# The last group of down products and the final norm in column chunks of 512, 512 and 26 instead of three of 350

## The chip, the cores and the metric

The kernel runs on one core of a Trainium2 chip. The metric is the device time of one execution in microseconds, the median of several. Engines are named TensorE (PE in the profile; PEld for its weight loads), VectorE (DVE), ScalarE (ACT), GpSimd (POOL) and SyncE (SP, which only issues transfers).

## The reference

One step of a decoder layer with D = 1024 for 1,050 tokens at once: 16 meta tokens, 1,024 prompt tokens, 8 sample tokens and 2 columns of padding. After two mixing branches (RG-LRU and gated linear attention) and their output projection comes the feed-forward part, and then the final norm. The change touches only the end of this:

```python
xn2 = rmsnorm(x, norm2_g)
u = xn2 @ w_ffn_up                      # 1024 -> 6144
uc = causal depthwise conv(u)
gate, val = split(uc, 2)
x = x + (gelu(gate) * val) @ w_ffn_down # 3072 -> 1024
y = x * rsqrt(mean(x * x) + 1e-6) * final_norm_g
```

All is float32. The outputs are y and the states of the branches and convolutions.

## The kernel before, in words

Activations are kept with the model dimension on the partitions: a block is 128 dimensions x C = 1050 token columns of float32, and the model dimension makes KB = 8 blocks. Every large product is made of three float32r products (high x high, high part of the weights x low part of the data, low x high), since weights and data are split into a high and a low part. GpSimd splits the weights (L366, L368), SP loads them (512 KB units). Columns go in three chunks of NW = 350, one PSUM bank each: `acc` is two groups of three banks, and two small banks are left, `sb6` and `sb7`.

The feed-forward part goes in 8 groups of GRP = 3 blocks of d_ff. For each group `up` makes gate and value, VectorE and ScalarE form the activation, and `down` adds the group's product to the residual X2, one 1050-column block at a time (L399 by way of `tile_products`; the add is L1502). The down products of the last group are done differently, and this is the part that changes. Their weights stand in SBUF split in full (`lhi`, `llo`, 3 units), so the loops are turned: columns outside, blocks inside. Chunk n = 0, 1, 2; in it block m = 0..7; in it 3 x 3 products of 350 columns (L737), into one bank per block (`last_bank(m)`, 8 banks). What follows is pipelined behind it by semaphores:

- VectorE adds the bank to X2 (L1540), and one block later adds the square to the running sum `ysum` (L1535; a copy, L1532, for block 0). These stand in one order in VectorE's program: add of block t, then sum of block t - 1.
- ScalarE squares the new X2 into one of two halves of `ysq` (L1092) and writes X2 x final_norm_g to Y (L1093).
- TensorE sums `ysum` over the partitions with a product by a matrix of ones, in fp32 (L422, called by `final_sum`). For chunk n - 1 this stands in TensorE's program after block 2 of chunk n, for the last chunk after its end. A bank is written again in chunk n once the add of the same block of chunk n - 1 is done; block 7 also waits for the Ln of chunk n - 1, because the ones product uses its bank.
- ScalarE makes the factor `yrs` (Ln, L1081, and Exp, L1084), in its program after block 2 of the next chunk.
- The scale Y x yrs is done by GpSimd for chunks 0 and 1, 8 blocks each (L391), and by VectorE for chunk 2 (L1551), after all its sums.
- SP stores y: one transfer for all 8 blocks of chunk 0, one for chunk 1 (L351), each after GpSimd's 8 scales, then four of two blocks for chunk 2 (L354). SP's program is in this order, and each transfer is queued behind the ones before it. At the end SP waits for all stores.

A row of y in memory is 1,050 floats, so a store of a chunk is made of one piece per partition and block, as long as the chunk is wide: 1,400 bytes for 350 columns.

Of the kernel before, what the change touches and what calls it, by code (L numbers as in the profile page):

```python
# [28 lines left out]
P = 128  # L29
D = 1024  # L30
# [24 lines left out]
EPS = 1e-6  # L55
TINY = 2.0 ** -63


# [44 lines left out]
def build(nc, I, O):  # L103
    ctx = ExitStack()
    with ctx:
# [105 lines left out]
        Y = at("y", M0, KB * C)  # L211
        ysq, ysum, yrs = at("y_square", F0, 2 * NW), at("y_square_sum", F0 + TB, C), at("y_rms", F0 + 2 * TB, C)

# [100 lines left out]
        def _(sp):  # L314
# [33 lines left out]
            Y3, y_out = Y.rearrange("p (k c) -> p k c", k=KB), O["y"].rearrange("k p c -> p k c")  # L348
            for n in range(2):
                sp.wait_ge(y_pool_done, KB * (n + 1))  # L350
                sp.dma_start(y_out[:, :, n * NW:(n + 1) * NW], Y3[:, :, n * NW:(n + 1) * NW]).then_inc(y_stored, 16)  # L351
            for k in range(0, KB, 2):
                sp.wait_ge(y_done, k + 2)
                sp.dma_start(y_out[:, k:k + 2, 2 * NW:], Y3[:, k:k + 2, 2 * NW:]).then_inc(y_stored, 16)  # L354
            sp.wait_ge(y_stored, 16 * (2 + KB // 2))
            sp.wait_ge(stored, 16 * 6)
# [3 lines left out]
        def _(pool):  # L360
# [25 lines left out]
            for n in range(2):  # L386
                c = slice(n * NW, (n + 1) * NW)
                pool.wait_ge(r3_done, n + 1)
                for m in range(KB):
                    pool.wait_ge(yg_done, KB * n + m + 1)  # L390
                    nc.gpsimd.tensor_tensor(blk(Y, m)[:, c], blk(Y, m)[:, c], yrs[:, c], ALU.mult).then_inc(y_pool_done, 1)  # L391

        @block.tensor
        def _(pe):
# [326 lines left out]
            def final_sum(n):  # L721
                pe.wait_ge(sum3_done, KB * (n + 1))
                pe.wait_ge(last_added, KB * (n + 1))
                norm_sum(ysum, n, last_bank(KB - 1), sum3_mm)
            for n in range(3):
                for m in range(KB):
                    if n == 0 and m in (2, 5):
# [5 lines left out]
                    for k in range(GRP):  # L733
                        v, t = divmod(m * GRP + k, KB)
                        b = (GRP + k) * C + n * NW
                        for w, x, a, z in ((lhi, AH, k == 0, False), (lhi, AL, False, False), (llo, AH, False, k == GRP - 1)):
                            mm = nc.tensor.matmul(last_bank(m)[:, 0:NW], w[v][:, t * P:(t + 1) * P], x[:, b:b + NW],  # L737
                                                  start=a, stop=z)
# [6 lines left out]
        def _(act):  # L745
# [332 lines left out]
            def final_factor(n):  # L1078
                c = slice(n * NW, (n + 1) * NW)
                act.wait_ge(sum3_mm, n + 1)  # L1080
                nc.scalar.activation(yrs[:, c], last_bank(KB - 1)[:, 0:NW], ACT.Ln, scale=1.0 / D, bias=cst[:, 0:1])\  # L1081
                    .then_inc(lnr3_done, 1)
                act.wait_ge(lnr3_done, n + 1)
                nc.scalar.activation(yrs[:, c], yrs[:, c], ACT.Exp, scale=-0.5).then_inc(r3_done, 1)  # L1084
            for n in range(3):
                c = slice(n * NW, (n + 1) * NW)
                for m in range(KB):
                    t = KB * n + m
                    act.wait_ge(last_added, t + 1)
                    if t >= 2:  # L1090
                        act.wait_ge(sum3_done, t - 1)
                    nc.scalar.activation(ysq[:, t % 2 * NW:(t % 2 + 1) * NW], blk(X2, m)[:, c], ACT.Square).then_inc(sq3_done, 1)  # L1092
                    nc.scalar.activation(blk(Y, m)[:, c], blk(X2, m)[:, c], ACT.Identity, scale=par("gf", m)).then_inc(yg_done, 1)  # L1093
                    if n > 0 and m == 2:
                        final_factor(n - 1)
# [3 lines left out]
        def _(dve):  # L1099
# [427 lines left out]
            def square_sum(t):  # L1527
                n, m = divmod(t, KB)
                c, q = slice(n * NW, (n + 1) * NW), ysq[:, t % 2 * NW:(t % 2 + 1) * NW]
                dve.wait_ge(sq3_done, t + 1)  # L1530
                if m == 0:
                    nc.vector.tensor_copy(ysum[:, c], q).then_inc(sum3_done, 1)  # L1532
                else:
                    dve.wait_ge(sum3_done, t)
                    nc.vector.tensor_tensor(ysum[:, c], ysum[:, c], q, ALU.add).then_inc(sum3_done, 1)  # L1535
            for n in range(3):
                c = slice(n * NW, (n + 1) * NW)
                for m in range(KB):
                    dve.wait_ge(last_mm, KB * n + m + 1)
                    nc.vector.tensor_tensor(blk(X2, m)[:, c], last_bank(m)[:, 0:NW], blk(X2, m)[:, c], ALU.add)\  # L1540
                        .then_inc(last_added, 1)
                    if KB * n + m > 0:
                        square_sum(KB * n + m - 1)
                if n < 2:
                    continue
                square_sum(3 * KB - 1)

                dve.wait_ge(r3_done, 3)
                for m in range(KB):
                    dve.wait_ge(yg_done, KB * n + m + 1)  # L1550
                    nc.vector.tensor_tensor(blk(Y, m)[:, c], blk(Y, m)[:, c], yrs[:, c], ALU.mult).then_inc(y_done, 1)  # L1551

# [110 lines left out]
```

## Time and profile before

| what | value |
|---|---|
| median of 3 runs | 1990.11 us (1988.91 to 1990.44) |
| profiled execution: span | 1984.4 us |
| profiled execution: own time | not given apart from the span |
| mean granted TensorE clock | 0.989 of full |
| moved by DMA | 127.38 MB |

Times in the profile are microseconds from the span's start, on the one core. A line such as "L737 PE MATMUL acc<-act_hi,last_hi" is the line of the kernel, the engine, the operation and the names of output and inputs; "x54" is how many. A product's duration is longer than its spacing to the next, since they overlap in the array; spacings of starts tell the pace. A TensorE product in fp32 is recorded as two instructions. PEclk is the granted TensorE clock (1.00 is 2.4 GHz, 0.50 is 1.2 GHz).

### The profile page before, as it was taken

What the parts mean: (1) busy time and instruction counts of PE and PEld (TensorE: products, weight loads), DVE (VectorE), ACT (ScalarE), POOL (GpSimd) and SP (SyncE); (2) the same over time, 40 slices, a digit from 0 to 9 for tenths busy, and PEclk for the clock granted to TensorE, in tenths of its full rate; (3) what the DMA queues carried; (4) which work ended last, traced back from release to release, by engine and by line L of the source; (5) the groups of instructions that cost most, each with busy time, mean ns of one, the idle gap of its engine ahead of it and who ended that gap; (6) DMA issues with size and microseconds to landing.
All of it is one profiled execution on the core that took longest, in us unless ns stands there. A gap on an engine that the chain in (4) does not pass through costs nothing.

```text
span 1984.4 us, 29047 instructions
## 1 busy us (share of the span) xinstructions
PE 1932.3 (97%) x11890; PEld 1904.1 (96%) x11890; DVE 911.0 (46%) x918; ACT 422.9 (21%) x480; POOL 702.0 (35%) x324
## 2 busy tenths in 40 slices
PE   7999999999999999999999999999999999999997
PEld 6999888888889999999999999999999999999997
DVE  5211277877865311141234455536253535354546
ACT  4000154555532100020021221101010201010115
POOL 2333222322234333343443333334333333333353
PEclk9999999999999999999999999999999999999999
DMA  5221123222211111131122111111111111111112
GB/s 191 86 89 43 44 97 110 77 90 77 77 68 49 49 47 42 56 127 42 42 80 103 55 43 43 54 43 43 44 54 43 43 44 53 44 43 43 54 51 87
DMA packets 48167, 127.38 MB, mean 64 GB/s; under 512 B 6952, under 2 KB 19880, under 8 KB 48080
## 3 DMA queue, kind: packets, MB, share of 16 engines
q1 hardware_dynamic: 27744, 88.52, 13.5%
q10 hardware_dynamic: 20352, 37.78, 5.4%
q8 instruction: 61, 1.00, 0.2%
q14 instruction: 10, 0.08, 0.0%
HBM read 108.23 MB, written 18.31 MB: 64 GB/s over the span
## 4 chain that ended last, share of the span: by engine, by line
PE 92%; DVE 4%; issue 3%; ACT 1%; DMA 0%; DVEq 0%; SPq 0%
PE acc L399 84%; PE acc L576 1%; PE acc L737 1%; PE small L496 1%; PE small L499 1%; DVE rg_xc_h L1307 1%; PE small L508 1%; DVE rg_xc_h L1304 1%; PE small L471 0%; DVE rg_ext L1129 0%; PE small L737 0%; PE small L589 0%; DVE gla_bc_keT L1194 0%; DMA x_in<-in_x 0%; PE small L515 0%
## 5 line engine op out<-in xcount | busy, mean ns | idle before, releaser
L366 POOL TENSOR_TENSOR w_hi<-w_raw,ones 128x1024 fp32r<-128x1024 f32 x149 | 288.0, 1933 | 1232.2 <-PE acc L399 1220.5
L399 PE MATMUL acc<-xn_hi,w_hi 128*128 128x350 f32 x2520 | 558.9, 330 | 15.2 <-DVE xn_lo L1117 11.2
L399 PE MATMUL acc<-xn_lo,w_hi 128*128 128x350 f32 x2520 | 546.7, 325 | 0.0
L399 PE MATMUL acc<-xn_hi,w_lo 128*128 128x350 f32 x2520 | 544.1, 324 | 0.0
L399 PEld LDWEIGHTS acc<-xn_hi,w_hi 128*128 128x128 f32 x2520 | 430.4, 191 | 21.0 <-issue 13.1
L399 PEld LDWEIGHTS acc<-xn_lo,w_hi 128*128 128x128 f32 x2520 | 432.7, 190 | 0.0
L399 PEld LDWEIGHTS acc<-xn_hi,w_lo 128*128 128x128 f32 x2520 | 432.1, 190 | 0.0
L368 POOL TENSOR_TENSOR w_lo<-w_raw,w_hi 128x1024 fp32r<-128x1024 f32 x149 | 384.3, 2579 | 11.7
L1502 DVE TENSOR_TENSOR residual<-acc,residual 128x1050 f32<-128x1050 f32 x56 | 70.0, 1250 | 117.0 <-PE acc L399 117.0
L1473 DVE SCALAR_TENSOR_TENSOR tmp<-val_ext,ffn_params,tmp 128x1040 f32<-128x1040 f32 x48 | 98.1, 2044 | 39.8 <-ACT tmp L1049 37.0
L1473 DVE SCALAR_TENSOR_TENSOR gate_conv<-gate_ext,ffn_params,gate_conv 128x1040 f32<-128x1040 f32 x48 | 92.1, 1920 | 41.0 <-ACT gate_conv L1043 38.1
L399 PE MATMUL acc<-act_hi,w_hi 128*128 128x350 f32 x504 | 108.9, 325 | 0.0
L399 PE MATMUL acc<-act_lo,w_hi 128*128 128x350 f32 x504 | 108.4, 323 | 0.0
L399 PE MATMUL acc<-act_hi,w_lo 128*128 128x350 f32 x504 | 108.2, 323 | 0.0
L1129 DVE TENSOR_TENSOR tmp<-acc,rms 128x1050 f32<-128x1050 f32 x24 | 30.0, 1251 | 150.9 <-PE acc L399 150.9
L1043 ACT ACTIVATE gate_conv<-gate_ext,ffn_params 128x1050 f32<-128x1050 f32 x24 | 30.4, 1267 | 291.4 <-DVE gate_ext L1469 291.4
L399 PEld LDWEIGHTS acc<-act_lo,w_hi 128*128 128x128 f32 x504 | 86.1, 189 | 0.0
L399 PEld LDWEIGHTS acc<-act_hi,w_hi 128*128 128x128 f32 x504 | 85.3, 189 | 0.5
L399 PEld LDWEIGHTS acc<-act_hi,w_lo 128*128 128x128 f32 x504 | 85.8, 189 | 0.0
L1469 DVE TENSOR_TENSOR val_ext<-acc,rms 128x1050 f32<-128x1050 f32 x24 | 30.0, 1251 | 104.6 <-PE acc L399 104.6
L1469 DVE TENSOR_TENSOR gate_ext<-acc,rms 128x1050 f32<-128x1050 f32 x24 | 30.0, 1251 | 88.7 <-PE acc L399 81.3
L1055 ACT ACTIVATE act_hi<-tmp 128x1050 fp32r<-128x1050 f32 x24 | 26.0, 1083 | 146.8 <-DVE tmp L1487 146.8
(218 smaller groups left out, 2089.4 us busy)
## 6 DMA issues: line engine op xcount, KB each, us to landing
w_raw<-in_w SPq DMA_DIRECT2D x153, 512.0 KB, 3.4
ha_scratch<-rg_gelu_ha ACTq DMA_DIRECT2D x8, 525.0 KB, 3.6
h<-ha_scratch ACTq DMA_DIRECT2D x8, 525.0 KB, 6.3
residual<-in_x ACTq DMA_DIRECT2D x8, 525.0 KB, 6.4
gla_qk_pair<-qk_scratch ACTq DMA_DIRECT2D x8, 512.0 KB, 5.8
smp_v_rows<-smp_v_scratch ACTq DMA_DIRECT2D x8, 512.0 KB, 6.5
out_gla_sample<-smp_state ACTq DMA_DIRECT2D x8, 512.0 KB, 3.8
smp_state<-in_gla_state ACTq DMA_DIRECT2D x7, 512.0 KB, 5.1
```

The lines of the kernel that those rows point to most:

```text
L366: nc.gpsimd.tensor_tensor(whi[s], raw[s], one, ALU.mult).then_inc(w_hi_done[s], 1)
L368: nc.gpsimd.tensor_tensor(wlo[s], raw[s], whi[s].bitcast(F32), ALU.subtract).then_inc(w_split[s], 1)
L399: mm = nc.tensor.matmul(accv[g][:, n], w[s][:, t * P:(t + 1) * P], x[:, n * NW:(n + 1) * NW], start=a, stop=z)
L496: mm = nc.tensor.matmul(bank[:, q * w:(q + 1) * w], vtm[0:w, s0:s0 + P], am[0:w, h * w:(h + 1) * w], start=True, stop=not inter)
L499: mm = nc.tensor.matmul(bank[:, q * w:(q + 1) * w], S[:, s0:s0 + P], qs[:, h * w:(h + 1) * w], start=False, stop=True)
L508: mm = nc.tensor.matmul(bank[:, (h % 2) * DV:(h % 2 + 1) * DV], bc[0:w, h * DK:(h + 1) * DK], vtm[0:w, h * DV:(h + 1) * DV], start=True, s ...
L1043: nc.scalar.activation(cg, eg[:, 2:2 + C], ACT.Identity, scale=fpr[:, bass.ds(2 * UB + F, 1)], bias=fpr[:, bass.ds(3 * UB + F, 1)]).then_i ...
L1055: nc.scalar.activation(AH[:, b:b + C], act_t, ACT.Copy).then_inc(acth_done, 1)
L1129: nc.vector.tensor_tensor(view3(out), acc[g][0:n_part, :, 0:NW], view3(rms[0:n_part, :]), ALU.mult)\
L1469: nc.vector.tensor_tensor(view3(e_t[:, 2:2 + C]), accv[g], view3(rms), ALU.mult).then_inc(acc_free[g], 1)
L1473: nc.vector.scalar_tensor_tensor(c_t[:, 0:NT], e_t[:, t:t + NT], fpr[:, bass.ds(t * UB + off_b + F, 1)], c_t[:, 0:NT], ALU.mult, ALU.add). ...
L1502: nc.vector.tensor_tensor(view3(blk(X2, m)), accv[g], view3(blk(X2, m)), ALU.add).then_inc(acc_free[g], 1)
```

## The change

The three chunks become `YC`: columns 0 to 511, 512 to 1023, and the last 26. Product, add, square, identity, sum, ones product, Ln, Exp and scale all take the width of their chunk; the number of products (216) and of adds, squares, identities and sums (24 each) is the same. `ysq` becomes two halves of 512 columns. The scales are shared out anew: GpSimd does all 8 blocks of chunk 0 and blocks 0 to 3 of chunk 1 (`YPOOL = 4`); VectorE, after all sums, does blocks 4 to 7 of chunk 1 and all 8 of chunk 2. The stores are one transfer for chunk 0 (2.10 MB), two of two blocks (0.52 MB each) and one of four (1.05 MB) for chunk 1, and one for chunk 2 (0.11 MB, pieces of 104 bytes).

```diff
--- before.py
+++ after.py
@@ -54,6 +54,8 @@
 UW = 12
 EPS = 1e-6
 TINY = 2.0 ** -63
+YPOOL = 4
+YC = ((0, 512), (512, 512), (1024, C - 1024))
 
 
 U_QKV = 1
@@ -209,7 +211,9 @@
         llo = [at(f"last_lo{u}", B0 + 8192 * u + 4096, D, F32R) for u in range(GRP)]
         assert 8192 * GRP <= KB * CB
         Y = at("y", M0, KB * C)
-        ysq, ysum, yrs = at("y_square", F0, 2 * NW), at("y_square_sum", F0 + TB, C), at("y_rms", F0 + 2 * TB, C)
+        YW = YC[0][1]
+        ysq, ysum, yrs = at("y_square", F0, 2 * YW), at("y_square_sum", F0 + TB, C), at("y_rms", F0 + 2 * TB, C)
+        assert 8 * YW <= TB
 
         acc = [ctx.enter_context(nc.psum_tensor(f"acc{s}", [P, 3, 512], F32)) for s in range(2)]
         sb6 = ctx.enter_context(nc.psum_tensor("small6", [P, 512], F32))
@@ -346,13 +350,18 @@
             sp.wait_ge(vkept, FB)
             sp.dma_start(O["u_last"], ubuf).then_inc(stored, 16)
             Y3, y_out = Y.rearrange("p (k c) -> p k c", k=KB), O["y"].rearrange("k p c -> p k c")
-            for n in range(2):
-                sp.wait_ge(y_pool_done, KB * (n + 1))
-                sp.dma_start(y_out[:, :, n * NW:(n + 1) * NW], Y3[:, :, n * NW:(n + 1) * NW]).then_inc(y_stored, 16)
-            for k in range(0, KB, 2):
-                sp.wait_ge(y_done, k + 2)
-                sp.dma_start(y_out[:, k:k + 2, 2 * NW:], Y3[:, k:k + 2, 2 * NW:]).then_inc(y_stored, 16)
-            sp.wait_ge(y_stored, 16 * (2 + KB // 2))
+            c = slice(0, YC[1][0])
+            sp.wait_ge(y_pool_done, KB)
+            sp.dma_start(y_out[:, :, c], Y3[:, :, c]).then_inc(y_stored, 16)
+            c = slice(YC[1][0], YC[2][0])
+            for k in range(0, YPOOL, 2):
+                sp.wait_ge(y_pool_done, KB + k + 2)
+                sp.dma_start(y_out[:, k:k + 2, c], Y3[:, k:k + 2, c]).then_inc(y_stored, 16)
+            sp.wait_ge(y_done, KB - YPOOL)
+            sp.dma_start(y_out[:, YPOOL:, c], Y3[:, YPOOL:, c]).then_inc(y_stored, 16)
+            sp.wait_ge(y_done, 2 * KB - YPOOL)
+            sp.dma_start(y_out[:, :, YC[2][0]:], Y3[:, :, YC[2][0]:]).then_inc(y_stored, 16)
+            sp.wait_ge(y_stored, 16 * (3 + YPOOL // 2))
             sp.wait_ge(stored, 16 * 6)
             sp.wait_ge(sS_stored, 16 * NB)
 
@@ -384,9 +393,9 @@
                 nc.gpsimd.tensor_tensor(llo[v], raw[s], lhi[v].bitcast(F32), ALU.subtract).then_inc(w_split[s], 1)
 
             for n in range(2):
-                c = slice(n * NW, (n + 1) * NW)
+                c = slice(YC[n][0], YC[n][0] + YC[n][1])
                 pool.wait_ge(r3_done, n + 1)
-                for m in range(KB):
+                for m in range(KB if n == 0 else YPOOL):
                     pool.wait_ge(yg_done, KB * n + m + 1)
                     nc.gpsimd.tensor_tensor(blk(Y, m)[:, c], blk(Y, m)[:, c], yrs[:, c], ALU.mult).then_inc(y_pool_done, 1)
 
@@ -721,8 +730,10 @@
             def final_sum(n):
                 pe.wait_ge(sum3_done, KB * (n + 1))
                 pe.wait_ge(last_added, KB * (n + 1))
-                norm_sum(ysum, n, last_bank(KB - 1), sum3_mm)
+                c0, w = YC[n]
+                nc.tensor.matmul(last_bank(KB - 1)[:, 0:w], ones, ysum[:, c0:c0 + w], start=True, stop=True).then_inc(sum3_mm, 1)
             for n in range(3):
+                c0, w_n = YC[n]
                 for m in range(KB):
                     if n == 0 and m in (2, 5):
                         pe.wait_ge(acc_free[(m - 2) // 3], G_LAST[(m - 2) // 3])
@@ -732,9 +743,9 @@
                             pe.wait_ge(lnr3_done, n)
                     for k in range(GRP):
                         v, t = divmod(m * GRP + k, KB)
-                        b = (GRP + k) * C + n * NW
+                        b = (GRP + k) * C + c0
                         for w, x, a, z in ((lhi, AH, k == 0, False), (lhi, AL, False, False), (llo, AH, False, k == GRP - 1)):
-                            mm = nc.tensor.matmul(last_bank(m)[:, 0:NW], w[v][:, t * P:(t + 1) * P], x[:, b:b + NW],
+                            mm = nc.tensor.matmul(last_bank(m)[:, 0:w_n], w[v][:, t * P:(t + 1) * P], x[:, b:b + w_n],
                                                   start=a, stop=z)
                     mm.then_inc(last_mm, 1)
                     if n > 0 and m == 2:
@@ -1076,20 +1087,20 @@
             act.preload_act_table_set(LN_EXP)
 
             def final_factor(n):
-                c = slice(n * NW, (n + 1) * NW)
+                c = slice(YC[n][0], YC[n][0] + YC[n][1])
                 act.wait_ge(sum3_mm, n + 1)
-                nc.scalar.activation(yrs[:, c], last_bank(KB - 1)[:, 0:NW], ACT.Ln, scale=1.0 / D, bias=cst[:, 0:1])\
+                nc.scalar.activation(yrs[:, c], last_bank(KB - 1)[:, 0:YC[n][1]], ACT.Ln, scale=1.0 / D, bias=cst[:, 0:1])\
                     .then_inc(lnr3_done, 1)
                 act.wait_ge(lnr3_done, n + 1)
                 nc.scalar.activation(yrs[:, c], yrs[:, c], ACT.Exp, scale=-0.5).then_inc(r3_done, 1)
             for n in range(3):
-                c = slice(n * NW, (n + 1) * NW)
+                c = slice(YC[n][0], YC[n][0] + YC[n][1])
                 for m in range(KB):
                     t = KB * n + m
                     act.wait_ge(last_added, t + 1)
                     if t >= 2:
                         act.wait_ge(sum3_done, t - 1)
-                    nc.scalar.activation(ysq[:, t % 2 * NW:(t % 2 + 1) * NW], blk(X2, m)[:, c], ACT.Square).then_inc(sq3_done, 1)
+                    nc.scalar.activation(ysq[:, t % 2 * YW:t % 2 * YW + YC[n][1]], blk(X2, m)[:, c], ACT.Square).then_inc(sq3_done, 1)
                     nc.scalar.activation(blk(Y, m)[:, c], blk(X2, m)[:, c], ACT.Identity, scale=par("gf", m)).then_inc(yg_done, 1)
                     if n > 0 and m == 2:
                         final_factor(n - 1)
@@ -1526,29 +1537,33 @@
 
             def square_sum(t):
                 n, m = divmod(t, KB)
-                c, q = slice(n * NW, (n + 1) * NW), ysq[:, t % 2 * NW:(t % 2 + 1) * NW]
+                c, q = slice(YC[n][0], YC[n][0] + YC[n][1]), ysq[:, t % 2 * YW:t % 2 * YW + YC[n][1]]
                 dve.wait_ge(sq3_done, t + 1)
                 if m == 0:
                     nc.vector.tensor_copy(ysum[:, c], q).then_inc(sum3_done, 1)
                 else:
                     dve.wait_ge(sum3_done, t)
                     nc.vector.tensor_tensor(ysum[:, c], ysum[:, c], q, ALU.add).then_inc(sum3_done, 1)
+            def y_scale(n, m):
+                c = slice(YC[n][0], YC[n][0] + YC[n][1])
+                dve.wait_ge(yg_done, KB * n + m + 1)
+                nc.vector.tensor_tensor(blk(Y, m)[:, c], blk(Y, m)[:, c], yrs[:, c], ALU.mult).then_inc(y_done, 1)
+
             for n in range(3):
-                c = slice(n * NW, (n + 1) * NW)
+                c = slice(YC[n][0], YC[n][0] + YC[n][1])
                 for m in range(KB):
                     dve.wait_ge(last_mm, KB * n + m + 1)
-                    nc.vector.tensor_tensor(blk(X2, m)[:, c], last_bank(m)[:, 0:NW], blk(X2, m)[:, c], ALU.add)\
+                    nc.vector.tensor_tensor(blk(X2, m)[:, c], last_bank(m)[:, 0:YC[n][1]], blk(X2, m)[:, c], ALU.add)\
                         .then_inc(last_added, 1)
                     if KB * n + m > 0:
                         square_sum(KB * n + m - 1)
-                if n < 2:
-                    continue
-                square_sum(3 * KB - 1)
-
-                dve.wait_ge(r3_done, 3)
-                for m in range(KB):
-                    dve.wait_ge(yg_done, KB * n + m + 1)
-                    nc.vector.tensor_tensor(blk(Y, m)[:, c], blk(Y, m)[:, c], yrs[:, c], ALU.mult).then_inc(y_done, 1)
+            square_sum(3 * KB - 1)
+            dve.wait_ge(r3_done, 2)
+            for m in range(YPOOL, KB):
+                y_scale(1, m)
+            dve.wait_ge(r3_done, 3)
+            for m in range(KB):
+                y_scale(2, m)
 
 
 def weight_units(w_in, w_a, w_b, w_out, w_up, w_down):
```

## Rows read from the trace of the kernel before

**Rows 1.** The page: the span, and its section 1 (busy time, share, instructions).

```profile
span 1984.4 us, 29047 instructions
...
PE 1932.3 (97%) x11890; PEld 1904.1 (96%) x11890; DVE 911.0 (46%) x918; ACT 422.9 (21%) x480; POOL 702.0 (35%) x324
```

**Rows 2.** The chain of work that ended last, the page's section 4, by engine.

```profile
PE 92%; DVE 4%; issue 3%; ACT 1%; DMA 0%; DVEq 0%; SPq 0%
```

**Rows 3.** The same chain in order of time: start us, us, what.

```profile
1963.98 5.80 PE acc L737 x36
...
1970.24 1.26 DVE y_square_sum L1535
...
1973.77 0.87 PE acc L422 x2
...
1974.66 0.56 ACT y_rms L1081
...
1976.73 2.60 DVE y L1551 x6
```

**Rows 4.** Single microseconds: stretch, length, engines busy, PEclk, DMA share, GB/s.

```profile
1964.00:1965.00 1.00, 1.00 (x8) 1.00 (x8) 0.38 (x1) 1.00 (x3) 0.00 (x0) 1.00 1.02 374
...
1974.00:1975.00 1.00, 0.62 (x2) 0.06 (x1) 0.00 (x0) 0.34 (x1) 0.38 (x1) 0.97 0.00 0
1975.00:1976.00 1.00, 0.00 (x0) 0.00 (x0) 0.23 (x1) 0.71 (x2) 0.00 (x0) 0.50 0.65 239
...
1983.00:1984.00 1.00, 0.00 (x0) 0.00 (x0) 0.00 (x0) 0.00 (x0) 0.00 (x0) 0.50 0.28 92
```

**Rows 5.** The stores of y: issues of L351, and KB each, us to landing.

```profile
L351 SPq DMA_DIRECT2D out_y<-y x2: 378/385/392, 1962.2 to 1974.4; - x2
...
out_y<-y SPq DMA_DIRECT2D x2, 1400.0 KB, 6.1
```

**Rows 6.** Timeline of chunk 0 and the start of chunk 1.

```profile
1935.11 0.33 PE L737 MATMUL small<-act_hi,last_hi 128*128 128x350 f32 x1
...
1950.87 0.32 PE L737 MATMUL acc<-act_hi,last_lo 128*128 128x350 f32 x1
...
1951.03 0.75 PE L422 MATMUL acc<-y_square_sum,ones 128*128 128x350 f32 x2
1951.23 0.52 DVE L1540 TENSOR_TENSOR residual<-acc,residual 128x350 f32<-128x350 f32 x1 [0.68 <-PE acc L737]
...
1953.81 8.39 POOL L391 TENSOR_TENSOR y<-y,y_rms 128x350 f32<-128x350 f32 x8 [24.24 <-ACT y_rms L1084]
```

**Rows 7.** Lines L1535 and L391, min/median/max ns, and one sum on the timeline.

```profile
L1535 DVE TENSOR_TENSOR y_square_sum<-y_square_sum,y_square x21: 511/516/1264, 1940.1 to 1972.7; 128x350 f32<-128x350 f32 x21
...
L391 POOL TENSOR_TENSOR y<-y,y_rms x16: 797/1087/1228, 1953.8 to 1973.3; 128x350 f32<-128x350 f32 x16
...
1967.34 1.02 DVE L1535 TENSOR_TENSOR y_square_sum<-y_square_sum,y_square 128x350 f32<-128x350 f32 x1
```

**Rows 8.** Groups with shapes kept apart, and a 512-column fp32 product in the chain.

```profile
L1240 DVE TENSOR_TENSOR gla_z_g_osq<-gla_z_g_osq 128x512 f32<-128x512 f32 x8 | 5.5, 683 | 0.0
...
L842 ACT ACTIVATE gla_z_g_osq<-v_o 128x512 f32<-128x512 f32 x4 | 2.5, 631 | 12.4 <-DVE v_o L1226 12.4
...
L1092 ACT ACTIVATE y_square<-residual 128x350 f32<-128x350 f32 x24 | 11.9, 498 | 35.2 <-DVE residual L1540 35.0
...
267.00 0.86 PE small L515 x2
```

**Rows 9.** Weight loads on the timeline, around 16 products with one moving column.

```profile
243.47 1.91 PEld L568 LDWEIGHTS small<-smp_qk,smp_state 128*128 128x128 f32 x16
245.31 0.46 PEld L399 LDWEIGHTS acc<-xn_hi,w_hi 128*128 128x128 f32 x3
```

**Rows 10.** DMA queue q10 in 42.9 to 47.0 us, then in 128.0 to 132.5 us.

```profile
q10 hardware_dynamic: 144, 0.54, 32.1%
...
q10 hardware_dynamic: 2080, 0.11, 32.4%
```

## The prediction

> **What bounds the kernel now.** I read the page first: TensorE is busy for 97% of a span of 1984.4 us [rows 1] and makes up 92% of the chain of waits [rows 2]. So a change in the last stage pays only if it shortens TensorE's work there or what lies behind its last product. I followed the chain in order of time [rows 3]. L737's products run without a gap to 1969.8. Behind them come square sums on VectorE, the ones product L422 at 1973.77, Ln and Exp on ScalarE, and eight scales on VectorE that end at 1979.3. The span ends 5 us later. The reader is to see that the chain leaves something out: what the DMA engines do. In single microseconds [rows 4] they idle in 1974 to 1975, start at about 1975.3, run at share 1.0 and end at 1983.3 (239 and 92 GB/s in the first and last microsecond, of 360). That is 2.87 MB in 8.0 us, 360 GB/s. The reason stands in the issues [rows 5]: chunk 0's store (1.43 MB) went out at 1962.2, was moved at 374 GB/s under the products and had landed 6.1 us later, so it cost nothing. Chunk 1's went out at 1974.4, when GpSimd had done its scales, and chunk 2's queued behind it. So the end is set by when the second store is handed over and by the bytes still unmoved then.
>
> The profiled execution's own time is not given apart from its span; I work on the span, 5.7 us below the median of 1990.1, and add the difference to that median.
>
> **Part 1: products of 512 columns.** From 1935.11 to the ones product at 1951.03 [rows 6] are 99 products (72 of chunk 0, 27 of chunk 1): 0.1608 us each. No row shows this form at 512 columns. Lower bound: 512 columns at 2.4 GHz with the 2 ns a pass that the fp32 product of 512 columns shows (two at 0.86 us, each two cycles a column [rows 8]), 0.216 us. Upper bound: in proportion, 0.1608 x 512/350 = 0.235. The row holds 145.8 ns of columns and 15 ns beside; I take those 15 as paid once per product, as each has one weight load: 0.2283. The 99 products then take 22.6 us instead of 15.9, and end at 1957.7.
>
> The Trainium skill, TensorE: Matmul & The Clock Gate, Back-to-back issue gap, gives columns / 2.4 + 2.5 ns for a warm product. For 350 columns that makes 148 ns, and the row has 161: the trace disagrees. By the rule the sum below would be 1.8 us less.
>
> **Part 2: to GpSimd's first scale.** Today it is 2.94 us from the last product of block 2 (1950.87) to the scale (1953.81) [rows 6], through add, square, identity, Ln and Exp. For 162 columns more, VectorE's op grows by 0.17 us (516 to 683) and ScalarE's by 0.13 (498 to 631) [rows 7, 8]; with four ScalarE steps and the product itself that is 0.8 us. The factor comes at 1961.3, 7.5 us later than now.
>
> **Part 3: GpSimd's scales.** Eight take 8.39 us [rows 6]. They alternate with VectorE: a sum (two operands in SBUF) takes 0.51 us alone and up to 1.26 while GpSimd runs, and GpSimd's 0.80 becomes 1.2 [rows 7]. All parts of this grow with the columns: 8.39 x 512/350 = 12.3. Chunk 0's scales end at 1973.5, and its store, now 2.10 MB, goes out then. Today 1.43 MB have already been moved by that time; that cover is gone.
>
> **Part 4: transfers.** From 1973.5 + 0.9 (issue to first byte, as 1974.4 to 1975.3 [rows 4, 5]) 4.19 MB are to be moved in rows of 2,048 bytes. Rows of 1,400 bytes go at 360 GB/s [rows 4], rows of 4,200 at 408 (0.54 MB in 32.1% of 4.1 us [rows 10]); I take 385: 10.9 us, to 1985.3. Chunk 2 is 1,024 rows of 104 bytes. 2,080 such small ones (loads, and some a little longer) held 32.4% of 16 engines for 4.5 us [rows 10], 11.2 ns each: 64 per engine, 0.8 us with their bytes. Bounds: 0.3 us by bytes alone, 2.4 us if small stores cost three times the loads. The span ends 1.1 us after the last byte (1983.3 to 1984.4 [rows 4]): 1987.2 on this path, +2.8.
>
> The Trainium skill, DMA: Bandwidth & Descriptors, opening table, says that under 512 bytes a transfer does a read-modify-write. It has no price for it, and no row here shows a store of rows this short.
>
> **Part 5: the path through chunks 1 and 2.** TensorE goes on at 1957.7 with a ones product of 0.86 (was 0.59) and 45 products of chunk 1: 1968.8. Chunk 2 has 72 products of 26 columns. No row has this form either. The nearest is 16 products with one column and a full 128x128 load: their loads start at 243.47 and the next unit's at 245.31, 0.115 us each [rows 9]. Upper bound 0.161, if today's spacing were the load's and not the columns'; under 0.115 nothing is gained, as will be seen. The first 27 take 3.1 us, to 1971.9. The ones product of chunk 1 also waits for block 7's sum, which with block 6's waits twice for a GpSimd scale of up to 1.2 us: about 1972.7. Ln starts 1.2 us later, Ln and Exp take 1.35: factor at 1975.3. GpSimd's four scales of chunk 1 then run to 1980.1. TensorE ends at 1973.6 + 45 x 0.115 = 1978.8. VectorE's eight short sums (0.1 us) wait for one scale of GpSimd each, so the last ends with GpSimd at about 1980.1: this hides TensorE's pace. Then VectorE does blocks 4 to 7 of chunk 1, 4 x 0.61 = 2.4 (0.44 spacing now, 0.17 more): 1982.5; SP is queued behind that wait, and chunk 2's store behind SP. Store of 1.05 MB: first byte 1983.4, moved 1986.1. Chunk 2's factor (1981.2) and eight scales (0.8 us, to 1983.3) are earlier than the DMA queue. Then 0.8 and 1.1: **1988.0**, 3.6 us late. This path is longer than part 4's by 0.8 us and sets the sum.
>
> Nothing is added elsewhere: SP goes from 6 stores of y to 5, at about 0.4 us of issue each, hidden by the waits; ScalarE keeps 54 instructions, two thirds of them longer, below TensorE's 2.05 us per block.
>
> **Sum.** +3.6 us on 1990.1: 1993.7. A measurement of this kernel can tell about 0.2%, 4.0 us, from no change. The sum lies just inside, so the two sides are nearly even.
>
> **Rivals.** (a) Short products are dearer. Below about 0.12 us TensorE hides behind GpSimd in chunk 2; this is the point from which it decides. At 0.161 TensorE ends at about 1981.9 and the sum is +5.4: 1995.5. At 0.23 (load and columns twice, as fp32 products run as two) it is +10: 2000. For it: no row of this form. Against: one-column products at 0.115 [rows 9]. Slower; 14%. (b) The stores of 104 bytes cost 2.4 us instead of 0.8, or the long rows move at 360: +4.5 to +5.4, 1995; 8%. (c) The wide products run at 0.216, transfers at 408: everything from 1957.7 on is 1.2 us earlier and the moves shorter: +1.2, 1991.3; 8%. The rule of part 1 is half of this one. (d) The shorter tail pays as meant: what follows the last product shrinks to little. It would need chunk 0's store under TensorE's work, but that is handed over only at 1973.5, with 4.3 MB to go; 3% for a gain over 0.2%.
>
> **Numbers.** Forecast (parts 1 to 5, with 0.216 to 0.235 and the alternation of part 3 uncertain by 1 us) +1.8 to +5.0, 67%; of it about 25 points lie over +4.0. Slower: 25 + 14 + 8 = 47%. Same: 42 + 8 = 50%. Faster: 3%. Range 1991.0 to 1998.5: from case (c) to the middle of (a). The forecast's own range is 1991.9 to 1995.1.
>
> **What would show it.** L737 at 512 columns spaced 0.228, at 26 columns 0.115; GpSimd's first scale at 1961.3, its eighth ending at 1973.5; store of chunk 0 issued then; sums of chunk 2 in step with GpSimd's scales; DMA share 1.0 from 1974.4 to about 1986, with hardly a gap; TensorE's last L737 at 1978.8. Wrong would be: short products over 0.13 us and VectorE's last adds behind TensorE; chunk 0's scales done before 1971; a DMA queue idle for over 1 us after 1975; or a last store of several us.

## The result and the profile after

The changed kernel takes 1998.44 us (median of 5 runs, 1995.44 to 2003.36), the kernel before 1989.92 (1986.25 to 1990.44): ratio 1.0044, 95% interval 1.0029 to 1.006, so 8.5 us slower. Forecast were 1993.7 us and, by a small margin, no change that a measurement can tell.

The profiled execution of the changed kernel is its slowest run, 2003.36 us with a span of 2001.5. Not all of the 17 us between the two spans is the change's. The last group's first product starts at 1935.11 in the profile before [rows 6] and at 1942.57 here, and in the profiles below anywhere from 1934.7 to 1941.1, though nothing ahead of it was changed. The granted clock of the stretch from 200 to 600 us, where TensorE waits now and then, differs from execution to execution: it is 0.96 in the profile before and 0.93 in this one. So I measure the **last stage** from that first product to the span's end: 49.3 us before, 58.9 after. It does not contain what varies ahead of it. One kernel below was profiled twice, and its last stage took 54.5 and 54.7 us, so I read nothing into a few tenths.

The page and the timeline of the changed kernel (start us, us, engine, line, operation):

```profile
span 2001.5 us, 29047 instructions
...
1942.57 0.40 PE L748 MATMUL small<-act_hi,last_hi 128*128 128x512 f32 x1
...
1979.56 0.26 PE L748 MATMUL acc<-act_lo,last_hi 128*128 128x26 f32 x1
1979.67 0.26 PE L748 MATMUL acc<-act_hi,last_lo 128*128 128x26 f32 x1
1980.16 2.08 PE L734 MATMUL acc<-y_square_sum,ones 128*128 128x512 f32 x2 [0.23 <-DVE y_square_sum L1546]
...
1984.02 0.37 PE L748 MATMUL acc<-act_lo,last_hi 128*128 128x26 f32 x1
1984.23 0.37 PE L748 MATMUL acc<-act_hi,last_lo 128*128 128x26 f32 x1
...
1969.05 12.01 POOL L400 TENSOR_TENSOR y<-y,y_rms 128x512 f32<-128x512 f32 x8 [32.02 <-ACT y_rms L1095]
1983.70 4.60 POOL L400 TENSOR_TENSOR y<-y,y_rms 128x512 f32<-128x512 f32 x4 [2.65 <-ACT y_rms L1095]
```

Two things stand in it. GpSimd's first scale starts 26.5 us after the first product and the eighth ends at 38.5: forecast were 26.2 and 38.4. And the products of 26 columns are spaced 0.11 us up to 1979.7 and 0.213 from 1982 on. What goes with the doubling is seen in stretches (length, then busy time of PE, PEld, DVE, ACT and POOL, PEclk, DMA share, GB/s):

```profile
1976.00:1978.00 2.00, 2.00 (x17) 1.83 (x15) 1.87 (x3) 1.17 (x3) 2.00 (x3) 1.00 0.00 0
1978.00:1980.00 2.00, 1.93 (x18) 1.84 (x17) 1.99 (x3) 1.34 (x4) 2.00 (x2) 1.00 0.00 0
1980.00:1982.00 2.00, 1.84 (x3) 0.84 (x3) 1.36 (x5) 0.86 (x4) 1.05 (x1) 0.51 0.00 0
1982.00:1984.00 2.00, 2.00 (x11) 1.97 (x10) 0.00 (x1) 1.32 (x2) 0.30 (x1) 0.50 0.99 380
...
1990.00:1992.00 2.00, 1.64 (x8) 1.54 (x8) 0.32 (x3) 0.51 (x3) 0.00 (x0) 0.50 0.29 111
1992.00:1994.00 2.00, 0.63 (x2) 0.50 (x2) 1.84 (x4) 0.84 (x4) 0.00 (x0) 0.50 0.00 0
1994.00:1996.00 2.00, 0.00 (x0) 0.00 (x0) 1.51 (x10) 0.00 (x0) 0.00 (x0) 0.50 0.15 57
1996.00:1998.00 2.00, 0.00 (x0) 0.00 (x0) 0.00 (x0) 0.00 (x0) 0.00 (x0) 0.50 0.99 361
1998.00:2000.00 2.00, 0.00 (x0) 0.00 (x0) 0.00 (x0) 0.00 (x0) 0.00 (x0) 0.50 0.66 159
```

The seventh number is the point: the granted clock falls from 1.00 (2.4 GHz) to 0.50 (1.2 GHz) at 1980, after 27 products of 26 columns and a gap of half a microsecond, and stays there. TensorE looks busy all the while, 3.93 of the 4 us before the fall: busy time does not tell how many columns it streams. The last two numbers answer to [rows 4]: the DMA engines do nothing from about 1991 to 1995.6, which is not the picture of a kernel that waits for bytes. The chain of waits says what they wait for, and the stores how long they take (KB each, us to landing):

```profile
1946.94 12.53 PE acc L748 x54
...
1982.23 9.42 PE acc L748 x45
...
1992.86 1.28 DVE y L1550 x2
...
1994.75 0.77 DVE y L1550 x8
```

```profile
out_y<-y SPq DMA_DIRECT2D x1, 2048.0 KB, 7.6
out_y<-y SPq DMA_DIRECT2D x2, 512.0 KB, 3.2
out_y<-y SPq DMA_DIRECT2D x1, 1024.0 KB, 4.4
out_y<-y SPq DMA_DIRECT2D x1, 104.0 KB, 5.6
```

54 wide products take 12.53 us, 0.232 each. The 45 of 26 columns behind the ones product take 9.42 us (45 x 0.115 = 5.2 was forecast), then come VectorE's wide scales, then 1.05 MB, then the small store.

### The profile page after: what moved, and what is told of

Same layout as the page of the kernel before. It is cut to its first block, busy times and chain, and to the rows that moved or that the text cites. A ratio compares the mean times of both kernels' runs of the same rounds, so it can differ in the third digit from the quotient of the medians.

```text
span 2001.5 us, 29047 instructions
## 1 busy us (share of the span) xinstructions
PE 1952.6 (98%) x11890; PEld 1916.6 (96%) x11890; DVE 912.5 (46%) x922; ACT 423.1 (21%) x480; POOL 702.0 (35%) x320
## 4 chain that ended last, share of the span: by engine, by line
PE 92%; DVE 4%; issue 3%; ACT 1%; DMA 0%; DVEq 0%; SPq 0%
PE acc L408 83%; PE acc L748 2%; PE acc L585 1%; PE small L505 1%; PE small L508 1%; PE small L517 1%; DVE rg_xc_h L1318 1%; DVE rg_xc_h L1315 1%; PE small L480 0%; DVE rg_ext L1140 0%; PE small L598 0%; DVE gla_bc_keT L1205 0%; PE small L748 0%; DMA x_in<-in_x 0%; PE small L524 0%
```

## The experiments

The theory at the start: the wide chunks and GpSimd behave as forecast, and the loss beyond the forecast is the clock. The rivals: a 26-column product is dear by itself; or the new sharing of scales and stores is at fault. All lengths below are of the last stage, the span's end less the start of the group's first product.

| kernel | first product | span | last stage |
|---|---|---|---|
| before | 1935.11 | 1984.4 | 49.3 |
| changed | 1942.57 | 2001.5 | 58.9 |
| 128 columns streamed in the last chunk | 1939.11 | 1993.6 | 54.5 |
| the same, profiled again | 1938.73 | 1993.4 | 54.7 |
| the same, without the last store | 1938.90 | 1991.4 | 52.5 |
| widths alone | 1934.73 | 1994.6 | 59.9 |
| sharing and stores alone (350, 350, 350) | 1937.09 | 1986.8 | 49.7 |
| changed, VectorE's scales interleaved | 1939.73 | 1996.8 | 57.1 |
| 128 columns and interleaved | 1938.19 | 1994.0 | 55.8 |
| the same, chunk 0 stored in four | 1940.09 | 1995.7 | 55.6 |
| before, chunk 1 stored in four | 1937.60 | 1985.2 | 47.6 |
| 350s, new sharing, last chunk stored in four | 1939.94 | 1987.7 | 47.8 |
| 414, 412, 224, the same | 1941.10 | 1990.0 | 48.9 |
| 350s, GpSimd 8 + 6, stored in four and four | 1937.41 | 1984.4 | 47.0 |

**1. The clock by itself.**

```diff
-                        b = (GRP + k) * C + c0
+                        wide = max(w_n, 128)
+                        b = (GRP + k) * C + c0 + w_n - wide
...
-                            mm = nc.tensor.matmul(last_bank(m)[:, 0:w_n], w[v][:, t * P:(t + 1) * P], x[:, b:b + w_n],
+                            mm = nc.tensor.matmul(last_bank(m)[:, 0:wide], w[v][:, t * P:(t + 1) * P], x[:, b:b + wide],
...
-                    nc.vector.tensor_tensor(blk(X2, m)[:, c], last_bank(m)[:, 0:YC[n][1]], blk(X2, m)[:, c], ALU.add)\
+                    nc.vector.tensor_tensor(blk(X2, m)[:, c], last_bank(m)[:, max(128 - YC[n][1], 0):max(128, YC[n][1])], blk(X2, m)[:, c], ALU.add)\
```

> The changed kernel, but the 72 products of the last chunk stream the last 128 columns instead of the last 26 (102 of them computed again and not used); VectorE reads the 26. All lengths are taken from the first product of the last group to the span's end: 49.3 us in the kernel before, 58.8 in the changed one. Theory A (the short products let TensorE's clock fall to 1.2 GHz, and everything behind them is late for that reason): the granted clock stays at 1.00 until the last product, these products are spaced 0.107 to 0.12 us instead of 0.21, and the length falls to about 53. Rival B (a product that writes so few columns is dear by itself once its bank and weights alternate, whatever the clock): if B holds through the load alone, spacing stays near 0.2 and the length at 58 to 59. Rival C (GpSimd and VectorE are what holds the chunk back): spacing falls, length stays above 57.

Measured: 54.5 us, 4.4 less than the changed kernel. Its stretches with the last bytes of its last store (columns as above), and from the timeline three of VectorE's short sums (the first while GpSimd has no work), two products, and VectorE's scales:

```profile
1976.00:1978.00 2.00, 1.81 (x11) 1.20 (x10) 1.91 (x5) 0.67 (x4) 1.60 (x2) 1.00 0.00 0
1978.00:1980.00 2.00, 2.00 (x21) 2.00 (x19) 0.45 (x4) 1.72 (x5) 0.50 (x1) 1.00 0.70 274
1980.00:1982.00 2.00, 2.00 (x21) 2.00 (x19) 1.99 (x6) 0.86 (x4) 2.00 (x3) 1.00 1.03 385
1982.00:1984.00 2.00, 0.80 (x8) 0.66 (x6) 1.99 (x4) 0.86 (x4) 2.00 (x2) 1.00 1.02 378
...
1990.50:1991.00 0.50, 0.00 (x0) 0.00 (x0) 0.00 (x0) 0.00 (x0) 0.00 (x0) 0.50 0.91 195
1991.00:1991.50 0.50, 0.00 (x0) 0.00 (x0) 0.00 (x0) 0.00 (x0) 0.00 (x0) 0.50 0.88 125
1991.50:1992.00 0.50, 0.00 (x0) 0.00 (x0) 0.00 (x0) 0.00 (x0) 0.00 (x0) 0.50 0.04 4
```

```profile
1978.92 0.18 DVE L1547 TENSOR_TENSOR y_square_sum<-y_square_sum,y_square 128x26 f32<-128x26 f32 x1
...
1979.07 0.28 PE L749 MATMUL acc<-act_lo,last_hi 128*128 128x128 f32 x1
1979.18 0.28 PE L749 MATMUL acc<-act_hi,last_lo 128*128 128x128 f32 x1
...
1980.93 0.94 DVE L1547 TENSOR_TENSOR y_square_sum<-y_square_sum,y_square 128x26 f32<-128x26 f32 x1
...
1981.97 1.12 DVE L1547 TENSOR_TENSOR y_square_sum<-y_square_sum,y_square 128x26 f32<-128x26 f32 x1
...
1984.36 3.26 DVE L1551 TENSOR_TENSOR y<-y,y_rms 128x512 f32<-128x512 f32 x12
```

The same 72 instructions with the same waits and five times the columns keep the clock at 1.00 to the last of them, and are spaced 0.111 us, where those of 26 columns are 11 in 2 us. So a product of 26 columns costs its weight load, 0.111, as long as the clock lasts; the form itself is not dear. The Trainium skill, TensorE: Matmul & The Clock Gate, Part 1, says that the clock is granted by how busy the array has lately been. The busy time in the profile does not tell the two kernels apart: PE has 3.93 of 4 us in 1976 to 1980 in the changed kernel, where the clock fell, and 3.81 of the same four here, where it stayed.

Nor is it the half microsecond without a product, ahead of the ones product: it is in both kernels. In the two other kernels with 26 columns (parts 2 and 4) the clock fell before that product, after some 23 products without a gap. Those of part 4, for TensorE alone (stretch, length, busy time, PEclk, DMA share, GB/s):

```profile
1976.20:1976.40 0.20, 0.20 (x5) 1.00 0.00 0
1976.40:1976.60 0.20, 0.20 (x4) 0.79 0.00 0
1976.60:1976.80 0.20, 0.20 (x3) 0.50 0.00 0
```

So with 26 columns the clock fell in three kernels of three. With 128, and with the 224 of part 6, the products are just as far apart and it fell in none. Where between 26 and 128 columns that changes, and why, stays open.

Of the way from 49.3 to 54.5 that remains, these lines show a part: a sum of 26 columns, 0.18 us alone, takes 0.9 to 1.2 beside GpSimd's scales, so the last sum ends at 1984.4, 45.3 us after the first product (forecast: 45.0), with TensorE long done. The Trainium skill, SBUF — State Buffer, Who interferes with whom, has the rule that a VectorE instruction with two SBUF inputs and a GpSimd instruction that reads SBUF shut each other out; the trace agrees.

The same kernel, timed twelve times:

> The changed kernel with 128 columns streamed in the last chunk, timed in rounds. Its profile gave 54.5 us from the group's first product to the end, 5.2 above the kernel before and 4.4 below the changed one. Theory A: a time 5 us above the kernel before (ratio 1.0026), where the changed kernel had 1.0044; if the clock were not the cause, 1.0044 again.

Measured: 1995.36 us (12 runs, 1991.42 to 1998.95) against 1989.0 of the kernel before on that chip (23 runs, 1985.8 to 1994.6), ratio 1.0028, interval 1.0016 to 1.0039. The last stage in its profile is 54.7 us. It fits theory A (1.0026). Its interval overlaps that of the changed kernel (from 1.0029), so the timed runs alone don't separate the two; the last stage in the profiles does.

**2. Which half of the change.** First the sharing and the stores alone:

```diff
-YC = ((0, 512), (512, 512), (1024, C - 1024))
+YC = ((0, 350), (350, 350), (700, C - 700))
```

> The changed kernel with chunks of 350, 350 and 350 again, so that only the new sharing of the scales (GpSimd 8 + 4, VectorE 4 + 8) and the new stores (8; 2, 2, 4; 8 blocks) are left of the change. Theory A (the widths are at fault): length from the first product of the last group to the end about 50 us, within 1.5 of the kernel before (49.3); a single last store of 1.43 MB ends it. Rival C (sharing and stores are at fault): 53 us or more.

Measured: 49.7 us, and one time of 1988.60 against 1988.44. The sharing costs next to nothing. Then the widths alone (stores and sharing as in the kernel before):

```diff
-YPOOL = 4
+YPOOL = 8
...
-            for k in range(0, YPOOL, 2):
-                sp.wait_ge(y_pool_done, KB + k + 2)
-                sp.dma_start(y_out[:, k:k + 2, c], Y3[:, k:k + 2, c]).then_inc(y_stored, 16)
-            sp.wait_ge(y_done, KB - YPOOL)
-            sp.dma_start(y_out[:, YPOOL:, c], Y3[:, YPOOL:, c]).then_inc(y_stored, 16)
-            sp.wait_ge(y_done, 2 * KB - YPOOL)
-            sp.dma_start(y_out[:, :, YC[2][0]:], Y3[:, :, YC[2][0]:]).then_inc(y_stored, 16)
+            sp.wait_ge(y_pool_done, 2 * KB)
+            sp.dma_start(y_out[:, :, c], Y3[:, :, c]).then_inc(y_stored, 16)
+            for k in range(0, KB, 2):
+                sp.wait_ge(y_done, k + 2)
+                sp.dma_start(y_out[:, k:k + 2, YC[2][0]:], Y3[:, k:k + 2, YC[2][0]:]).then_inc(y_stored, 16)
...
-            dve.wait_ge(r3_done, 2)
-            for m in range(YPOOL, KB):
-                y_scale(1, m)
```

> The chunks of 512, 512 and 26 alone: the scales shared out as in the kernel before (GpSimd 8 + 8, VectorE the last chunk) and the stores as there (8; 8; four of two blocks). Theory A (the widths carry the loss): TensorE's clock falls to 1.2 GHz in the last chunk as in the changed kernel, GpSimd's second eight scales end 50.4 us after the group's first product, and the 2.10 MB behind them end the span: length 59 to 60.5, no better than the changed kernel's 58.9. Rival (the new sharing causes part of the loss): below 57.

Measured: 59.9 us. Its second eight scales and two of its stretches:

```profile
1975.85 9.16 POOL L398 TENSOR_TENSOR y<-y,y_rms 128x512 f32<-128x512 f32 x8 [2.64 <-ACT y_rms L1093]
```

```profile
1981.00:1983.00 2.00, 2.00 (x12) 2.00 (x11) 0.86 (x2) 0.43 (x2) 2.00 (x3) 0.50 0.00 0
...
1988.00:1990.00 2.00, 0.00 (x0) 0.00 (x0) 0.00 (x0) 0.00 (x0) 0.00 (x0) 0.50 1.02 378
```

GpSimd's scales end 50.3 us after the first product, and 2.10 MB follow them; the clock is low here too. So in these profiles the widths carry the whole loss, and the new sharing saves one microsecond of it.

**3. The last store.** The second kernel of part 1, with this left out as well:

```diff
-            sp.dma_start(y_out[:, :, YC[2][0]:], Y3[:, :, YC[2][0]:]).then_inc(y_stored, 16)
-            sp.wait_ge(y_stored, 16 * (3 + YPOOL // 2))
+            sp.wait_ge(y_stored, 16 * (2 + YPOOL // 2))
```

> The changed kernel with 128 columns streamed in the last chunk, and without the last store, that of the last 26 columns (1,024 pieces of 104 bytes), so y is incomplete in the output. With it the length was 54.5 us. The DMA engines moved those pieces in 0.85 us, and the span ended 2.1 us after the last byte, not 1.1 as behind long pieces. If that is the small store's own cost: 52.6. If its cost is only the moving: 53.6.

Measured: 52.5 us, 2.0 less. The end of its transfers:

```profile
1990.00:1991.00 1.00, 0.00 (x0) 0.00 (x0) 0.00 (x0) 0.00 (x0) 0.00 (x0) 0.50 0.33 125
1991.00:1991.40 0.40, 0.00 (x0) 0.00 (x0) 0.00 (x0) 0.00 (x0) 0.00 (x0) 0.50 0.00 0
```

Here the last byte of long pieces moves at about 1990.35 and the span ends 1.1 us later, as in the kernel before. With the small store the bytes stop at 1991.5 (part 1) and the span ends 2.1 us later. So in this pair of kernels 1,024 pieces of 104 bytes cost 0.9 us of moving and 1.0 us of later completion. The second figure is not a constant: over all profiles of this case the span ends 1.5 to 2.5 us after the last byte where the small store is last, and 1.0 to 1.4 us where pieces of 1,400 or 2,048 bytes are, with 1.8 behind the 896 bytes of the kernel with 224 columns. The later completion would fit the read-modify-write under 512 bytes that the Trainium skill, DMA: Bandwidth & Descriptors, opening table, states; no run tells it from another cause.

**4. VectorE's order.** Its four wide scales moved between the last adds:

```diff
                     if KB * n + m > 0:
                         square_sum(KB * n + m - 1)
+                    if n == 2 and m >= YPOOL:
+                        dve.wait_ge(r3_done, 2)
+                        y_scale(1, m)
             square_sum(3 * KB - 1)
-            dve.wait_ge(r3_done, 2)
-            for m in range(YPOOL, KB):
-                y_scale(1, m)
```

> The changed kernel, but VectorE scales blocks 4 to 7 of chunk 1 one at a time behind the adds of blocks 4 to 7 of the last chunk, not after all sums. Theory A: TensorE's clock falls all the same (0.50 from about 37 us after the first product of the group), its last product ends at the same place (49 us after the first), but the store of 1.05 MB goes out some 5 us earlier and only the 0.1 MB store is left behind the last factor: length about 55.5 instead of 58.8. If nothing of the loss is in VectorE's order: 58 to 59.

Measured: 57.1 us: 1.9 less, of some 3.4 expected. The issue of the 1.05 MB store, in the changed kernel and here:

```profile
1994.78 0.37 SPq L361 DMA_DIRECT2D out_y<-y  x1
...
1989.76 0.37 SPq L361 DMA_DIRECT2D out_y<-y  x1
```

That is 52.2 and 50.0 us after the first product: the store goes out 2.2 us earlier, not 5, since the scale of block 7 stands behind the add of block 7, and that behind TensorE's last product. At the low clock TensorE takes 1.92 us a block, in which VectorE's other wide scales find room. With the clock kept:

> Both edits at once on the changed kernel: the last chunk streams 128 columns (clock kept), and VectorE scales blocks 4 to 7 of chunk 1 behind the adds of blocks 4 to 7 of the last chunk. With the clock kept the length from the first product of the last group to the end was 54.5 us, of which VectorE's four wide scales and the 1.05 MB store behind them are the end. Theory A (two causes, the clock 4.4 us and VectorE's late scales of chunk 1 some 3 us): 51 to 52. If VectorE's scales only change places with the sums and push those back: 54 or more.

Measured: 55.8 us, 1.3 more than without the interleaving; the expectation failed and its alternative holds. GpSimd's four scales, 4.60 us in the kernel with 128 columns alone, and the last sum:

```profile
1978.59 6.23 POOL L400 TENSOR_TENSOR y<-y,y_rms 128x512 f32<-128x512 f32 x4 [1.90 <-ACT y_rms L1096]
...
1985.38 0.17 DVE L1547 TENSOR_TENSOR y_square_sum<-y_square_sum,y_square 128x26 f32<-128x26 f32 x1
```

VectorE's wide scales take turns with GpSimd's, so they stretch both, and the last sum, which the last factor waits for, ends 47.4 us after the first product instead of 45.3. Early work that takes turns with another engine's was no free work.

**5. Are bytes the bound?** In the last kernel (128 columns and interleaved), chunk 0's store in four pieces as well:

```diff
-            sp.wait_ge(y_pool_done, KB)
-            sp.dma_start(y_out[:, :, c], Y3[:, :, c]).then_inc(y_stored, 16)
+            for k in range(0, KB, 2):
+                sp.wait_ge(y_pool_done, k + 2)
+                sp.dma_start(y_out[:, k:k + 2, c], Y3[:, k:k + 2, c]).then_inc(y_stored, 16)
```

> As the run with both edits, and chunk 0 of y stored in four pieces of two blocks, each behind its two scales. Theory A (the bytes of chunk 0 do not set the end, the DMA queue has gaps behind them): the length stays within 0.5 us of that run. Rival (the DMA queue is the bound, as part 4 of the prediction has it): with chunk 0 handed over 9 us earlier the length falls by 1.5 us or more.

Measured: 55.6 against 55.8 us. No: 2.10 MB handed over late cost nothing there, and in the kernel of 55.8 us the DMA share is down to 0.43 from 1984 to 1986, behind them. It was not run on the changed kernel itself, whose DMA engines idle for over 4 us behind those bytes. In the kernel before:

```diff
-            for n in range(2):
-                sp.wait_ge(y_pool_done, KB * (n + 1))
-                sp.dma_start(y_out[:, :, n * NW:(n + 1) * NW], Y3[:, :, n * NW:(n + 1) * NW]).then_inc(y_stored, 16)
+            sp.wait_ge(y_pool_done, KB)
+            sp.dma_start(y_out[:, :, 0:NW], Y3[:, :, 0:NW]).then_inc(y_stored, 16)
+            for k in range(0, KB, 2):
+                sp.wait_ge(y_pool_done, KB + k + 2)
+                sp.dma_start(y_out[:, k:k + 2, NW:2 * NW], Y3[:, k:k + 2, NW:2 * NW]).then_inc(y_stored, 16)
```

> The kernel before, with chunk 1 of y stored in four pieces of two blocks, each behind its two scales, instead of in one. The reading of the kernel before was that its end is set by bytes waiting for the DMA engines (2.87 MB from 1975.3 on), not by the chain of engines. If so, the DMA engines start about 6 us earlier, the last store is alone behind VectorE's last scale, and the length falls from 49.3 to about 47.7 us. If the chain of engines alone sets the end: 49.3.

Measured: 47.6 us. Yes: there the reading of [rows 4] was right.

**6. Towards a version shorter than both.** Chunks of 350 with the new sharing, the last chunk stored in four pieces:

> Chunks of 350, the new sharing of scales (GpSimd 8 + 4, VectorE 4 + 8) and the new stores, but chunk 2 stored in four pieces of two blocks as in the kernel before. The same with one last store of 1.43 MB took 49.7 us from the first product of the group to the end. If that store's 4 us of moving behind the last scale is the end: 46.7. If something else holds it: 48.5 to 49.7.

Measured: 47.8 us, between the two that were expected. In its trace the DMA engines still have a queue behind them (length, PE busy, PEclk, DMA share, GB/s):

```profile
1981.00:1983.00 2.00, 0.00 (x0) 0.50 1.02 360
1983.00:1985.00 2.00, 0.00 (x0) 0.50 1.02 358
```

Then other widths, `YC = ((0, 414), (414, 412), (826, C - 826))`:

> The same with chunks of 414, 412 and 224 columns. A pair of load and product takes 0.111 us at 128 columns (load bound) and about 15 ns above columns / 2.4 GHz when wider, so 224 columns (0.108 to 0.112) cost no more time per column than 350 and the granted clock should stay at 1.00. The last chunk's sum, factor, eight scales and stores are shorter. Expected length 45.7 us, against 46.7 for 350, 350, 350. Rival (GpSimd, with wider chunks, becomes the end): 47 or more.

Measured: 48.9 us, not 45.7. Behind its last product (stretches, and the chain):

```profile
1978.00:1980.00 2.00, 0.07 (x1) 0.00 (x0) 1.90 (x4) 1.40 (x4) 1.49 (x2) 0.98 0.76 267
1980.00:1982.00 2.00, 1.11 (x2) 0.50 (x2) 2.00 (x5) 0.53 (x2) 0.00 (x0) 0.50 0.57 211
```

```profile
1979.84 0.40 DVE y_square_sum L1547
1980.25 0.04 issue
1980.29 1.13 PE acc L735 x2
```

The last sum ends 39.1 us after the first product (37.7 with 350s), since the sums queue behind wider scales of GpSimd; TensorE is idle for two microseconds meanwhile, the clock falls, and the ones product of 224 columns takes 1.13 us where one of 350 takes 0.87. With 350s and GpSimd at 8 + 6 (`YPOOL = 6`):

> Chunks of 350; GpSimd scales 8 blocks of chunk 0 and 6 of chunk 1, VectorE the other two of chunk 1 and the last chunk; stores: chunk 0 whole, chunk 1 in four pieces of two blocks, chunk 2 in four. With GpSimd 8 + 4 the length was 47.8 us, and the end waited for bytes (0.72 and 1.43 MB behind each other). With 0.36 MB less handed over late: 46.9, and 2.4 us less than the kernel before in time, about 0.12%, hardly more than a measurement can tell. If bytes are not what ends it: 47.6 or more.

Measured: 47.0 us, and 1986.58 us (12 runs, 1983.2 to 1991.98) against 1989.0, ratio 0.9987, interval 0.9975 to 0.9999. As expected in both: 2.4 us faster than the kernel before, a gain smaller than the 0.2% that was called tellable, with an interval that ends just short of 1. Most of it is not the new sharing: the kernel before with nothing but its second store cut in four (part 5) has 47.6 us of the same 49.3.

## Why the prediction was wrong

It had +3.6 us; the time grew by 8.5, the last stage in the profiles by 9.6.

- **Part 1** (products of 512 columns): 0.2283 forecast, 0.232 measured (12.53 us for 54). The proportional bound 0.235 was as near. The Trainium skill's rule for it (TensorE: Matmul & The Clock Gate, Back-to-back issue gap), 216 ns, is 16 ns short of it here, and 13 ns at 350 columns: the trace disagrees.
- **Parts 2 and 3** (factor, GpSimd's scales, alternation with VectorE): right to 0.3 us.
- **Part 4** (transfers): pieces of 2,048 bytes move at 378 to 389 GB/s (385 forecast). The small store's 0.8 us of moving was 0.9, but it completes 1.0 us later than long pieces do, which had no term. Chunk 0's lost cover cost nothing in the kernel where it was tried.
- **Part 5** is the step that failed: "the nearest is 16 products with one column ... 0.115 us each" was taken from a stretch with the clock at 1.00 (243 to 246 us in the profile before), and the prediction has no word on the clock: it put the chance that it falls at nothing, without a reason. The load-bound cost was right (0.111), and the bound above it, 0.161, was called for the wrong reason. What came was 0.213, at half the clock, from 1980 on. Rival (a) had the size (0.23, +10 us), but with 14%, and a mechanism (load and columns twice) that does not occur; that its +10 lies near 9.6 is in part luck, since it puts 6.4 us on the short products, where the run gives 4.4. The claim that GpSimd hides TensorE's pace holds only below 0.12, as the text itself said.
- The 9.6 us then divide thus, two parts by a run and the third as the remainder: 4.4 us for the clock (58.9 to 54.5), 2.0 for the last store (54.5 to 52.5), and 3.2 (52.5 to 49.3) that no single edit takes away; the trace puts it on VectorE's sums and wide scales behind GpSimd and the 1.05 MB behind those. Forecast for the last two together were 3.6 us; they came to 5.2. Of the 1.6 more, 1.0 is the late completion and 0.3 the last sum; the rest is in terms of about 0.1 each.
- **Rows that could have warned**: [rows 4] show the clock at 0.97 and then 0.50 within four microseconds of the last L737 product. (That one starts at 1970.88; the 1969.8 of the prediction is only where the chain of waits leaves TensorE.) They show that the clock can change inside this stage, though behind idle time and not in a stream of products; the prediction reads their DMA columns and not that one.
- The shorter tail, what the change seems to aim at, did come: sum, factor and scales of the last chunk are short. But the tail is the last chunk's only if its predecessor is out of the way, and chunk 1's scales and 1.05 MB were not.

## What to carry to other kernels

When columns are re-cut, look at the thinnest piece: below the columns that hide a weight load it costs the load, and a run of such products can bring TensorE's clock down, which the profile shows in PEclk and not in busy time. If a thin remainder can't be avoided, try letting it stream more columns than it needs, as 128 in place of 26 did here. And a remainder's other costs don't shrink with it: each short VectorE sum waited for a whole scale of GpSimd's, and each short piece of a store has its own price.

## What the runs showed of the hardware

- Products of 26 and of 128 columns both take 0.111 us with their weight load at the high clock; 26 columns take 0.213 at the low one.
- The clock stayed at 1.00 through 72 products of 128 columns, and fell to 0.50 in all three kernels profiled with 26 columns (the changed one, the widths alone, the interleaved one), in two of them after some 23 products with TensorE busy throughout.
- Computing 102 columns again that nobody needs made the changed kernel's last stage 4.4 us shorter.
- The span ended 2.1 us after the last byte of 1,024 pieces of 104 bytes, and 1.1 us after that of long pieces in the same kernel without them; over all profiles it is 1.5 to 2.5 against 1.0 to 1.8 us.
